# A hybrid pooling and DeltaNet layer on one core: the prologue reordered and packed, and GpSimd's order inside a slot turned

## The reference, cut to what matters

```python
mod = silu(c) @ w_ada + b_ada                    # (9, 3072)
shift, scale, gate = split(mod, 3)
h = rms_norm(x, pre_norm_w) * (1 + scale) + shift
u_a, z_a, qkv, z_b, b, a = split(h @ w_in)       # 512, 512, 1536, 512, 4, 4
y_a = pool_mix(u_a) * silu(z_a)                  # sliding means of 2, 4, 8, 16, then a 128x128 mix
q, k, v = silu(causal_conv(qkv))                 # 4 taps; q and k then normalised
o, S = gated_delta_rule(q, k, v, exp(g), beta)   # chunks of 128, 4 heads of 128x128 state
y_b = rms_norm(o) * silu(z_b)
x = x + gate * rms_norm(concat(y_a, y_b) @ w_out, post_norm_w)
```

## Time and profile before

| what | value |
|---|---|
| median of three timed runs | 1092.45 us (1090.98 to 1092.65) |
| the profiled execution's own time | 1091.97 us |
| span of that execution, first to last instruction | 1090.2 us |
| busy: TensorE, VectorE, ScalarE, GpSimd | 1056.4, 652.1, 358.5, 223.1 us |
| DMA moved | 196.04 MB, 180 GB/s on average |
| mean granted TensorE clock | 0.992 of full |

### The profile page before, as it was taken

How to read it: one execution, slowest core, us unless ns; L and a number is a source line. 1 busy time by engine, 2 the same in 40 slices (tenths; PEclk the granted TensorE clock), 3 DMA queues, 4 the chain that set the end, 5 groups by cost and what they waited for, 6 DMA issues and landing times.

```text
span 1090.2 us, 16889 instructions
## 1 busy us (share of the span) xinstructions
PE 1056.4 (97%) x6301; PEld 831.8 (76%) x6301; DVE 652.1 (60%) x1389; ACT 358.5 (33%) x713; POOL 223.1 (20%) x226
## 2 busy tenths in 40 slices
PE   7999999989999999999999999999999999999995
PEld 1568767867878888887878888887878888788774
DVE  1569887546436795565356785565255776455644
ACT  3356421343624521132424511143325621122211
POOL 0233343653410011331000011231000010443000
PEclk9999999999999999999999999999999999999998
DMA  9587548434766454323646553224664344222265
GB/s 366 194 302 266 221 159 306 145 114 167 250 242 242 185 192 155 116 78 117 237 158 260 196 193 126 107 78 167 221 247 195 120 150 152 79 79 98 93 237 182
DMA packets 44964, 196.04 MB, mean 180 GB/s; under 512 B 8858, under 2 KB 9626, under 8 KB 27348
## 3 DMA queue, kind: packets, MB, share of 16 engines
q1 hardware_dynamic: 44884, 194.97, 49.1%
HBM read 150.14 MB, written 44.81 MB: 179 GB/s over the span
## 4 chain that ended last, share of the span: by engine, by line
PE 62%; DVE 3%; POOL 2%; issue 2%; ACT 0%; DVEq 0%; POOLq 0%; ACTq 0%
PE acc L2002 12%; PE acc L2004 11%; PE acc L2003 11%; PE ring L2044 7%; PE ring L2031 2%; PE ring L2032 2%; PE ring L2033 2%; PE acc L2031 2%; PE acc L2033 2%; PE acc L2032 2%; PE ring L2196 2%; PE ring L2061 1%; PE ring L2070 1%; PE ring L2071 1%; POOL win L1828 1%
## 5 line engine op out<-in xcount | busy, mean ns | idle before, releaser
L2002 PE MATMUL acc<-hhi,wsl 128*128 128x512 f32 x768 | 315.6, 411 | 1.1 <-DVE y L1290 1.1
L2004 PE MATMUL acc<-hhi,wsl 128*128 128x512 f32 x768 | 300.8, 392 | 0.0
L2003 PE MATMUL acc<-hlo,wsl 128*128 128x512 f32 x768 | 300.4, 391 | 0.0
L2002 PEld LDWEIGHTS acc<-hhi,wsl 128*128 128x128 f32 x768 | 144.9, 189 | 33.7 <-issue 5.1
L2004 PEld LDWEIGHTS acc<-hhi,wsl 128*128 128x128 f32 x768 | 144.5, 188 | 31.9
L2003 PEld LDWEIGHTS acc<-hlo,wsl 128*128 128x128 f32 x768 | 145.0, 189 | 27.1 <-issue 1.4
L1176 DVE SCALAR_TENSOR_TENSOR cacc<-raw,cw,cacc 128x512 f32<-128x512 f32 x144 | 114.6, 796 | 5.1
L1788 POOL TENSOR_TENSOR wsl<-wraw,wsl 128x512 fp32r<-128x512 f32 x64 | 87.1, 1378 | 136.3 <-ACT wsl L864 136.3
L893 ACT ACTIVATE raw<-acc 128x512 f32<-128x512 f32 x48 | 28.6, 597 | 153.5 <-PE acc L2004 153.4
L1086 DVE TENSOR_TENSOR hlo<-htmp,hhi 128x512 fp32r<-128x512 f32 x32 | 22.2, 692 | 62.2 <-ACT hhi L838 61.9
L1173 DVE TENSOR_SCALAR cacc<-raw,cw 128x512 f32<-128x512 f32 x48 | 23.5, 490 | 52.9 <-ACT raw L893 50.5
(11 more groups left out here) (305 smaller groups left out, 1774.4 us busy)
## 6 DMA issues: line engine op xcount, KB each, us to landing
wsl<-kept_w SPq DMA_DIRECT2D x96, 1024.0 KB, 4.8
kept_w<-wsl SPq DMA_DIRECT2D x32, 1024.0 KB, 6.4
wraw<-in_w SPq DMA_DIRECT2D x64, 256.0 KB, 3.5
wada<-in_w_ada SPq DMA_DIRECT2D x8, 1024.0 KB, 12.9
xb<-in_x SPq DMA_DIRECT2D x16, 512.0 KB, 5.8
xres<-in_x SPq DMA_DIRECT2D x16, 512.0 KB, 5.7
out_y<-ytok SPq DMA_DIRECT2D x16, 512.0 KB, 8.0
wada<-in_w_ada SPq DMA_DIRECT2D x16, 256.0 KB, 5.1
```

The lines of the kernel that those rows point to most:

```text
L2002: nc.tensor.matmul(acc[t % 2][:], w[:, 0, k], hi[:, k], start=(k == 0), stop=False)
L2003: nc.tensor.matmul(acc[t % 2][:], w[:, 0, k], lo[:, k], start=False, stop=False)
L2004: last = nc.tensor.matmul(acc[t % 2][:], w[:, 1, k], hi[:, k], start=False, stop=(k == KT - 1))
```

## The change

- **Load order.** x is loaded ahead of the first `w_ada` part; the second part comes after the small vectors and the gate weights; the raw weight halves come before the third and fourth parts.
- **Packing.** The nine silu(c) columns are widened to 32 (`cpad`, the rest zero) and the eight `k` steps of a `w_ada` part are dealt over three groups of 32 output partitions, `k % 3`. The copies take 96 rows, and the turning matmul multiplies by a 96x9 `fold` matrix that adds the three groups. The same packing is used for the gate rows.
- **Order on TensorE.** x is turned before the second `w_ada` part is multiplied; tiles 0 and 1 are interleaved by `k` and take their first four steps before the last one and a half parts are multiplied; the gate projection is done among the `k` steps of tile 0.
- **Other engines.** ScalarE scales two of the four x tiles. VectorE writes the low halves of weight tiles 0 and 1 in place of GpSimd. The sample rows' work on VectorE moves to tile 2 of block 0.
- **Gate rows.** ScalarE copies the packed sums out of PSUM in slot 1; VectorE adds three groups instead of one, in slots 3 and 4 instead of 1 and 2; TensorE spreads in slots 5 and 6.
- **GpSimd in a slot.** Output-norm root, x root, decayed state, sliding sums, low halves.

```diff
+GR = 3
-GATE_ROW = {1: 0, 2: 1}
-GROW_AT = {4: 0, 5: 1}
+GATE_COPY = 1
+GATE_ROW = {3: 0, 4: 1}
+GROW_AT = {5: 0, 6: 1}
...
# SyncE
+            for i in range(4):
+                sp.dma_start(xb[:, i], a["x"][0][:, i]).then_inc(x_in.sem, 16)
             modulation(0)
-            modulation(1)
...
+            # fold, ident; pool_scale, o_norm, a_log, dt_bias, w_gate
+            modulation(1)
...
             for n in range(WR):
                 raw_half(n)
+            sp.dma_start(xrow, a["xs"]).then_inc(sm_x0, 16)
+            modulation(2)
             modulation(3)
...
# ScalarE
-            nc.scalar.activation(cin[:], cin[:], ACT.Silu).then_inc(s_cact, 1)
+            nc.scalar.activation(cpad[:, :, 0:1 + NS], cin[:], ACT.Silu).then_inc(s_cact, 1)
             front_act(act, PROLOGUE)
+            act.wait_ge(*rx_f(PROLOGUE, 0))
+            for t in range(2, 4):
+                nc.scalar.activation(xb[:, t], xb[:, t], ACT.Copy, scale=rx[:, t:t + 1]).then_inc(xn.sem, 1)
...
+            halves_hi(0)
+            halves_hi(1, range(1))
             for hf in range(2):
-                halves_hi(hf)
+                if hf:
+                    halves_hi(1, range(1, 2))
                 act.wait_ge(s_half, 3 * (hf + 1))
...
+                    if it == 0 and slot == GATE_COPY:
+                        for m in range(2):
+                            act.wait_ge(s_gate, m + 1)
+                            nc.scalar.activation(cacc[0:GR * BS, m], bank("ada", m)[0:GR * BS, :], ACT.Copy).then_inc(s_ada, 1)
...
# VectorE
-                nc.vector.tensor_copy(rows9[j], acc[j % 2][0:1 + NS, :]).then_inc(s_rows, 1)
+                nc.vector.tensor_copy(rows96[j], mod_bank[j][0:GR * BS, :]).then_inc(s_rows, 1)
...
+            front_xn(dve, PROLOGUE, range(2))
+            row_copy(0)
...
+            first_lo(0)
+            row_copy(1)
+            first_lo(1)
+            first_lo(2)
+            dve.wait_ge(s_prm, 32)
+            first_factors(0)
+            for m in range(3):
+                first_halves(m)
+            row_copy(2)
+            first_halves(3)
...
+            row_copy(3)
+            first_lo(3)
+            first_factors(1)
+            for m in range(4, 8):
+                first_halves(m)
...
+                for g in range(GR):
...
+                    nc.vector.tensor_tensor(grow[:, cols], grow[:, cols], cacc[g * BS:g * BS + 1 + NS, m], ALU.add
...
# GpSimd
-            for t in range(WS - 1):
-                halves_lo(t)
...
-                    for n in parts:
-                        if n <= PARTS and n % 8 == 0:
-                            split_lo(it, NQ + n // 8)
-                    if sc is not None and q == 0:
...
-                        nc.gpsimd.tensor_tensor(sdec[:], st[:], bc(eg[:, 1, sc]), ALU.mult).then_inc(sdec_f.sem, 1)
                     if norm is not None and step_ == 1:
                         pool.wait_ge(*o_n(it, norm))
                         nc.gpsimd.tensor_tensor(on[:], on0[:], mhalf[:, 0:H], ALU.pow).then_inc(o_rt.sem, 1)
                     if slot == FRONT + 1 and not last:
                         front_rx(pool, it)
+                    if sc is not None and q == 0:
...
+                        nc.gpsimd.tensor_tensor(sdec[:], st[:], bc(eg[:, 1, sc]), ALU.mult).then_inc(sdec_f.sem, 1)
                     for n in parts:
                         if n % 8 == 7 and tile_kind(NQ + n // 8)[0] == "u":
                             u_tile(it, NQ + n // 8)
+                    for n in parts:
+                        if n <= PARTS and n % 8 == 0:
+                            split_lo(it, NQ + n // 8)
...
# TensorE
                 for k in range(e * KT // 2, (e + 1) * KT // 2):
-                    last = nc.tensor.matmul(acc[j % 2][0:1 + NS, :], cin[:, k, :], wada[j][:, k], start=(k == 0),
-                                            stop=(k == KT - 1))
+                    g = k % GR
+                    last = nc.tensor.matmul(mod_bank[j][g * BS:(g + 1) * BS, :], cpad[:, k], wada[j][:, k], start=(k < GR),
+                                            stop=(k >= KT - GR))
...
+            modulate(0, 0)
+            modulate(0, 1)
+            pe.wait_ge(s_ident, 32)
             for m in range(3):
                 front_pe(pe, PROLOGUE, m)
+            turn_rows(0)
+            modulate(1, 0)
+            modulate(1, 1)
+            turn_rows(1)
+            modulate(2, 0)
             front_pe(pe, PROLOGUE, 3)
...
+                for k in range(4):
+                    for t in range(2):
                         tile(0, t, k)
+                    if k == 1:
+                        modulate(2, 1)
+                turn_rows(2)
+                modulate(3, 0)
+                for m in range(4, 7):
+                    front_pe(pe, PROLOGUE, m)
+                modulate(3, 1)
...
+                gates(0, range(4))
+                turn_rows(3)
                 front_pe(pe, PROLOGUE, 7)
+                for k in range(4, KT):
+                    tile(0, 0, k)
+                    gates(0, range(k, k + 1))
+                for k in range(4, KT):
+                    tile(0, 1, k)
```

209 lines of the change are left out of this document (107 added, 102 removed).

## The result

| | median | runs | lowest to highest |
|---|---|---|---|
| before | 1092.45 us | 7 | 1089.97 to 1094.94 |
| after | 1086.11 us | 7 | 1084.71 to 1089.74 |

The ratio is 0.9944, 95% interval 0.9929 to 0.9960: 6.3 us faster. The forecast was 15.0 us faster, 1077.0, with a range up to 1085. The sign was right and the size was not; the time lies 1.1 us outside the range.

A forecast was written before the change was run, and what follows sets the result against it. TensorE was taken as the bound, busy 1056.4 of 1090.2 us. From 1091.97 us, the terms -7.0 - 1.6 - 3.6 + 1.0 - 5.9 + 2.1 = -15.0 gave 1077.0 us, range 1070 to 1085.

The forecast's parts named there:

- tile 2 at ~54.9: Prologue: the new schedule starts tile 2 at ~54.9 instead of 61.86, -7.0 us.
- -1.6 ... if nothing new stops TensorE just before: Tile 2: its first nine starts no longer at half clock, -1.6 us, provided no new TensorE stop stands just before.
- a wait until the fifth pair at ~46.5: Prologue schedule: after the gate matmuls, copy, turn and factors, TensorE waits for the fifth hi and lo pair until ~46.5.
- Packing: w_ada and gate-row matmuls: three column groups run side by side, half a part 1.7 us instead of 3.5.
- packing does not overlap: Rival: column groups gain no overlap, so prologue and gate-row gains are lost; 1089 us, chance 0.08.
- Gate rows: Block 0 gate rows: TensorE saves 8.7 us, VectorE's limit leaves -3.6; possible half clock at the new stop, +1.0.
- GpSimd's order, block 0: Block 0, last slots: sums end ~237.7 instead of 242.30; 5.9 of 7.54 lost us come back, -5.9.
- about 1.9 us of stall: Block 0: stall left as VectorE's chain ends late with low halves beside it, in place of block 1's 0.28.
- Blocks 1 and 2: GpSimd's state now stands between root and sums, so TensorE's wait grows by 1.05 us per block, +2.1 in all.
- The clock stays low in a prologue full of waits: Rival: TensorE has 1.2 GHz up to ~28, five packed halves and turns take longer, +7; 1084 us, chance 0.15.
- Gained in full: Rival: gate rows gain all, VectorE running faster away from GpSimd, -5 more and no half clock; 1071 us, chance 0.08.
- low halves late: Rival: split work last in each slot brings weight tiles after TensorE wants them, 5 us in block 0; 1082 us, chance 0.05.

The follow-up runs named there:

- all_unpacked: Changed kernel with packing taken away everywhere (one column group instead of three, 32 columns wide), order kept; 1101.77 us.
- fill_turn: Changed kernel with eight additional 512-column matmuls, results never read, behind the last turn of w_ada rows; 1086.58 us.
- turn_early: Changed kernel with the last turn of w_ada rows issued after two of the four gate-projection steps instead of behind all four; 1083.6 us.
- rows_split: Changed kernel with five of the six small VectorE sample-row operations moved behind the product gg that TensorE waits for at tile 3; 1085.63 us.
- gates_first: Changed kernel, block 0 alone: ScalarE's Abs, Exp, Ln for the gates and VectorE's sample rows and gg moved earlier, to tile 1; 1086.24 us.
- fill_gate: Changed kernel with matmuls that nothing reads in block 0, one ahead of tile 14 and three ahead of tile 15; 1084.72 us.
- zmul_early: Changed kernel with VectorE's zmul of tile 13 ahead of its last piece of the substitution, block 0 alone; 1092.01 us.
- gate_unpacked: Changed kernel with the gate rows' 16 matmuls on one column group as before, one group copied and added; 1090.3 us.
- lo_defer: Changed kernel with GpSimd's four low halves of slots 15 to 18, block 0, held back until VectorE's chain behind the sums is through; 1081.2 us.
- state_first: Changed kernel with GpSimd's decayed state computed ahead of the two roots; 1081.8 us.
- before_pool_new: The kernel before the change, with nothing but GpSimd's new order inside a slot; 1091.1 us.
- comb6: Changed kernel with `state_first`, `turn_early`, `lo_defer`, `fill_gate` and VectorE's scalings of the next x in slots 19 to 22 instead of 17 to 20; 1078.59 us.

## Why the prediction was right or wrong

**The step that failed** is the front part of the sum: "tile 2 at ~54.9", -7.0, and behind it "-1.6 ... if nothing new stops TensorE just before". Together 8.6 us were forecast and 2.5 came. The terms of the 6.1 us between them, each from a row:

- 2.2 us: the schedule's durations. The first projection starts at 29.01 and not 28.1. Then three halves took 1.90 and not 1.7, and two turns of rows that multiply by `fold` took 0.96 and not the 0.41 of the kernel before (second row below), 1.7 us; 0.4 of these 2.6 us must have lain in waits, since `k` step 4 of tile 0 came at 48.71 and not 46.5. The dearer turn is not the price of the 96 rows, for with one group it took 1.05 us in `all_unpacked`: four transposes (four records) have become four fp32 matmuls (eight records), and the forecast priced the old ones.
- 1.6 us: the half clock at 49.4 to 52.8. The schedule itself had "a wait until the fifth pair at ~46.5"; it priced the wait and not the clock behind it, although show just that. `fill_turn` and `turn_early` are without it. Four of the twelve profiles with the stop are without it too, so this term is there in most executions and not in all.
- 0.6 us: the wait for `gg` at tile 3, and 1.6 us: the half clock behind it. The forecast looked at VectorE's convolutions and found room; ScalarE's list it did not look at. The Ln ends 4.9 us behind the start of ScalarE's copy of tile 2 in both kernels, but TensorE now needs it earlier. The sample rows' operations did "move into a VectorE wait of tile 2", the one of 1.42 us in the first row below, but the convolution took 3.24 us and not 2.33, and they ended 0.4 us behind the Ln. `rows_split` shows the Ln as the bound that is left, `gates_first` removed the wait and the stretch.

```profile
74.21 0.18 DVE L1539 SCALAR_TENSOR_TENSOR gsp<-ga,gl 128x16 f32<-128x16 f32 x1 [1.42 <-ACT gl L981]
```

```profile
41.50 0.41 PE L1934 MATMUL ring<-ident,pooled 9*128 9x9 f32 x4 [0.77 <-DVE pooled L1103]
```

Behind the third term, and behind the gate rows, is one cause, and `gates_first`, `fill_gate` and `zmul_early` show it: in block 0 the engines that TensorE waits for have so little room that a stop that goes returns a few tiles on. The forecast argued so at the gate rows and not at tile 3.

**Packing** was right. Half a part took 1.90 us against a forecast of 1.7, the gate rows 5.34 against 5.2, and `all_unpacked` prices the whole at 15.7 us. That run is also the world of the rival "packing does not overlap", which the forecast put at 1089: it came to 1102. The Trainium skill, "TensorE: Matmul & The Clock Gate", Part 3, has a measured speedup of 2.38 times for three column tiles; 13.90/5.34 is 2.60 here, where eight steps fall on three groups as 3, 3, 2.

**Gate rows.** The mechanism was right, -2.6 forecast and -1.8 measured: TensorE saved 8.5 us, and the wait for VectorE that could move up gave the rest of the answer. `gate_unpacked` puts it at 1.45, `fill_gate` the half clock in it at 1.2 (forecast 1.0). That the 1.0 came out is in part luck: it holds for the stretch of 6.8 us in this profile, and one of 3.4 us costs nothing there.

**GpSimd's order, block 0.** The place was right, and the sums' end: forecast 237.7 less the shift of 4.3, measured 233.64. The size was not, -5.9 against -3.1. The term that was mis-sized is the "about 1.9 us of stall" for low halves that run beside VectorE's chain. The term took the stall from 0.28 to 1.9, 1.6 us more than in block 1; the window came out 4.4 us longer than block 1's, and 7.54 - 4.4 = 3.1. Of the 4.4, 2.4 are waits (2.72 in place of 0.28, since two operations were stretched and not one) and 1.6 are the half clock behind them, which the term did not have; the small rest no row here names. `lo_defer` recovers 3.1 of it.

**Blocks 1 and 2.** Right to 0.1 us, in mechanism and size: `state_first` removes it.

**The rivals.** "Packing does not overlap" fell. "The clock stays low in a prologue full of waits" came true in part: half clock for one half part ahead of the first projection in most profiles, and behind the stops near tile 0 and at tile 3, instead of a clock that is low throughout. Its 1084 lies nearer to the measured time than the forecast, but by luck: its mechanism, five halves and the turns at 1.2 GHz before ~28, is in none of the profiles. "Gained in full" and "low halves late" fell: no raw or low half ended a wait of TensorE.

**What stays open.** Why a stop of the same length has a half-clock stretch behind it in one execution and not in the next (a version with the stop and a clock held by other means was not tried); how much of block 0's limit is ScalarE and how much VectorE; and how much of the prologue's gain is the new order's, since packing was not tried in the old one.

## What to carry to other kernels

Before you count the time that a stop costs as won, list for each of the other engines when its next result would be ready if TensorE came earlier, ScalarE's table loads and copies included; where they are some 80% busy, as both were here between tiles 2 and 4, much of it comes back as the next wait. When two engines hold the same result within half a microsecond, moving one shows only the other. A stop of TensorE is priced with its clock: here about 1.6 us for a half-clock stretch of 3.4 us behind it, in part of the executions, and nothing where another engine is the bound anyway. In a strictly ordered queue the operation whose input is earliest goes first, and bulk work without a near reader goes where it runs beside nothing that is waited for: these two moves were worth 3.0 and 3.1 us here by the profiles (`state_first`, `lo_defer`), the packed gate rows 1.45.

## What the runs showed of the hardware that was not expected

- A wait of 0.60 us and a few matmuls with 1 to 128 columns (71.40 to 73.1) had a half-clock stretch behind them; a wait of 2.27 us in `before_pool_new` had none. The length of the wait alone does not tell.
- Matmuls that nobody reads, put into the waits at the gate rows, kept the clock up behind them: neither of the two profiles with them (`fill_gate`, `comb6`) has a half-clock stretch there, and all 14 with packed gate rows and without them do, 3.4 or 6.8 us long. Ten in the prologue took the median to 1084.46 us against 1086.11, four at the gate rows to 1084.72, eight at the last turn left it at 1086.58; the intervals of all three overlap with the changed kernel's.
- Column groups of three ran 2.60 times as fast as one (13.90 and 5.34 us). A turn of rows by four fp32 matmuls took 0.96 us with 96 rows and 1.05 with 32; the four transposes of nine rows had taken 0.41.
- A VectorE operation with two SBUF inputs took 1.76 us instead of 0.69 beside GpSimd's low halves, and a small one of 0.21 us (`gg`) took 1.2 in the eight profiles in which a low half ran beside it for 1.1 us.
